# Delta-rule levels on Trainium2: the second chunk's mask chain first, the third level's masks ahead of the samples' decay, and the sample queries as a second column of the key's product

## The reference

```
L = (k k^T) * exp(where(strict, b_i - b_j, -inf)) * beta_i
U, Wk = solve((L + I), [v * beta, k * beta * exp(b)])
P = (q k^T) * exp(where(causal, b_i - b_j, -inf))
W = U - Wk S ;  o = (q * exp(b)) S + P W ;  S = exp(b_last) S + (k * exp(b_last - b))^T W
```

## Time and profile before

| What | Value |
|---|---|
| Median of 3 runs | 2649.16 us |
| The profiled execution, its own time | 2651.1 us |
| Its span, first to last instruction | 2649.4 us |
| PE busy | 2594.3 us (98%) |
| DVE, ACT, POOL busy | 1254.7 us (47%), 819.1 us (31%), 303.7 us (11%) |
| DMA | 246.75 MB, mean 93 GB/s |
| Mean granted clock of TensorE | 0.989 of full speed |

### The profile page before, as it was taken

How to read it: one execution, slowest core, us unless ns; L and a number is a source line. 1 busy time by engine, 2 the same in 40 slices (tenths; PEclk the granted TensorE clock), 3 DMA queues, 4 the chain that set the end, 5 groups by cost and what they waited for, 6 DMA issues and landing times.

```text
span 2649.4 us, 48882 instructions
## 1 busy us (share of the span) xinstructions
PE 2594.3 (98%) x20695; PEld 2501.5 (94%) x20695; DVE 1254.7 (47%) x1578; ACT 819.1 (31%) x1042; POOL 303.7 (11%) x311
## 2 busy tenths in 40 slices
PE   8999999999999999999999999999999998999998
PEld 8999999898989899999999999989998998999998
DVE  5444324647464754443344442386457645444422
ACT  4222222324232432222222222253333334322222
POOL 1000001202020210000100000104420442000000
PEclk9999999999999999999999999999999999999999
DMA  4333233525252423322333323321122111333232
GB/s 135 90 95 85 79 106 124 187 80 187 80 187 80 150 82 95 95 80 88 103 104 83 95 79 96 99 80 35 49 78 73 35 49 52 83 92 95 76 89 76
DMA packets 340334, 246.75 MB, mean 93 GB/s; under 512 B 9428, under 2 KB 320908, under 8 KB 340208
## 3 DMA queue, kind: packets, MB, share of 16 engines
q1 hardware_dynamic: 325856, 197.32, 25.2%
q0 software_dynamic: 14352, 47.58, 5.0%
HBM read 218.81 MB, written 26.05 MB: 92 GB/s over the span
## 4 chain that ended last, share of the span: by engine, by line
PE 90%; DVE 5%; issue 2%; ACT 1%; POOL 1%; DMA 0%; DVEq 0%; SPq 0%; POOLq 0%; ACTq 0%
PE ps L744 60%; PE ps L931 16%; PE ps L1119 4%; PE ps L829 1%; PE ps L850 1%; PE ps L1059 1%; PE ps L1129 1%; POOL osum L589 1%; DVE xl L1661 1%; PE ps L1070 1%; PE ps L784 1%; DVE wl L1655 1%; PE ps L1100 0%; PE ps L1082 0%; PE ps L990 0%
## 5 line engine op out<-in xcount | busy, mean ns | idle before, releaser
L744 PE MATMUL ps<-xh,wh 128*128 128x260 f32 x2816 | 569.0, 283 | 2.7 <-DVE gate L2219 1.6
L744 PE MATMUL ps<-xh,wl 128*128 128x260 f32 x2816 | 568.1, 283 | 0.0
L744 PE MATMUL ps<-xl,wh 128*128 128x260 f32 x2816 | 567.4, 283 | 0.0
L1655 DVE TENSOR_TENSOR wl<-raw,wh 128x2048 fp32r<-128x2048 f32 (+1 forms) x204 | 427.5, 2096 | 267.9 <-ACT wh L1332 267.7
L1332 ACT ACTIVATE wh<-raw 128x2048 fp32r<-128x2048 f32 (+1 forms) x204 | 354.5, 1738 | 344.0 <-PE ps L744 190.0
L744 PEld LDWEIGHTS ps<-xh,wh 128*128 128x128 f32 x2816 | 435.4, 189 | 4.7 <-issue 2.3
L744 PEld LDWEIGHTS ps<-xh,wl 128*128 128x128 f32 x2816 | 435.0, 189 | 0.0
L744 PEld LDWEIGHTS ps<-xl,wh 128*128 128x128 f32 x2816 | 433.8, 189 | 0.0
L744 PE MATMUL ps<-hh,wh 128*128 128x260 f32 x1408 | 284.4, 283 | 0.0
L744 PE MATMUL ps<-hh,wl 128*128 128x260 f32 x1408 | 283.0, 282 | 0.0
L744 PE MATMUL ps<-hl,wh 128*128 128x260 f32 x1408 | 282.8, 282 | 0.0
(11 more groups left out here) (366 smaller groups left out, 2910.6 us busy)
## 6 DMA issues: line engine op xcount, KB each, us to landing
raw<-in_ffn_gu_dram SPq DMA_DIRECT2D x176, 512.0 KB, 4.9
raw<-in_ffn_down_dram SPq DMA_DIRECT2D x64, 384.0 KB, 3.6
raw<-in_ret_w_in_dram SPq DMA_DIRECT2D x48, 512.0 KB, 4.4
raw<-in_ffn_down_dram SPq DMA_DIRECT2D x64, 320.0 KB, 4.0
s_ring<-in_state_ret_dram POOLq DMA_DIRECT2D x32, 512.0 KB, 7.0
out_dram<-s_ring POOLq DMA_DIRECT2D x32, 512.0 KB, 3.1
raw<-in_gdn_w_in_dram SPq DMA_DIRECT2D x32, 512.0 KB, 4.5
raw<-in_ret_w_out_dram SPq DMA_DIRECT2D x16, 512.0 KB, 4.1
```

What stands on the lines that cost most here:

```text
L744: m_ = nc.tensor.matmul(ps[:, 2 * q + h, 0:HALF], w_, v[:, kt0 + t, h * HALF:(h + 1) * HALF], start=b_, stop=e_)
L1655: nc.vector.tensor_tensor(wl[:, s, 0:cols], raw[:, s, 0:cols], wh[:, s, 0:cols].bitcast(F32), ALU.subtract).then_inc(w_low, 1)
```

## The change

The diff has three parts. First, the second chunk of a pair: `n1` of it is made by DVE (before, by POOL); ACT makes `d1` before the key rows `kb`, `kd`; its `pt` and `qd` and PE's `qk` stand behind level 1 and the samples' key products. The first chunk's `qd` stands behind the second's `n2`. Second, POOL makes the masks of level 3 before it scales the first two states, and those of level 5 before the other two. Third, the samples' queries: DVE copies keys and queries side by side once for each head group (`kc`, `qc`) and multiplies them (`kq`); PE's product at level 1 takes both columns, and one product with ones sums `kq` over the rows; DVE builds the output from these (`sa`, `sd`, `so`), and the products `os` and copies `oz` are gone. Beside these, the output's `o` does all four products with the state first and waits for `W` behind them.

```
             if l == 1:
+                out += [f"{n}.{both[1]}" for n in odd.split()]
...
-    pairs((["0 dd n2 L l0 m0 pt qd", "1 dd n2 L l0", "0 a1", "1 m0", "0 a2", "1 pt qd"],
+    pairs((["0 dd n2 L l0 m0 pt", "1 dd n1 n2", "0 qd", "1 L l0", "0 a1", "1 m0", "0 a2"],
...
-    pairs((["0 n1 l1", "1 n1", "0 l2", "1 l1"], ["0 n1 l1", "1 n1", "0 l2", "1 l1"]), ["l"], ["s2"], {2: ("", (0, 1), "se"), 4: ("", (2, 3), "se")})]))
+    pairs((["0 n1 l1 l2", "1 l1"], ["0 n1 l1 l2", "1 l1"]), ["l"], ["s2"], {3: ("", (0, 1), "se"), 5: ("", (2, 3), "se")})]))
...
                             for h in range(GG):
-                                m_ = nc.tensor.matmul(ps[:, 1, h * GC + b % GC:h * GC + b % GC + 1], g_ring[:, b % RING, h, :],
-                                                      gk[:, h, SEQ + b:SEQ + b + 1], start=True, stop=True)
+                                o = 2 * (h * GC + b % GC)
+                                nc.tensor.matmul(ps[:, 5, o:o + 2], g_ring[:, b % RING, h, :], pairs_s[:, h, b, :], start=True, stop=True)
                         if step == 2:
+                            m_ = nc.tensor.matmul(ps[:, 5, 2 * GG * GC:3 * GG * GC].rearrange("p (h b) -> p h b", h=GG), ones[:],
+                                                  kq[:, :, GC * p:GC * p + GC], start=True, stop=True)
                             did(m_, f"r{p}")
...
-                            v(f"wc{p}" if l == 2 else f"oz{b - 2}")
+                            v((f"pt.{2 * p + 1}" if b % 2 else f"sd{p}") if l == 2 else f"kw{b - 2}")
                             rows_of(5 - 4 * (b % 2), lambda h: wt[:, h, b:b + 1], ident[:], f"wr{b}")
-                    if l in (3, 5) and step:
-                        for b in (GC * p + l - 4 + step,):
-                            v(f"sn{b}")
-                            for h in range(GG):
-                                m_ = nc.tensor.matmul(ps[:, 5 - 4 * (b % 2), h:h + 1], g_ring[:, b % RING, h, :],
-                                                      gq[:, h, SEQ + b:SEQ + b + 1], start=True, stop=True)
-                            did(m_, f"os{b}")
...
-                        v(f"W.{c}")
                         v(f"qd.{c}")
                         for h in range(GG):
-                            o = ps[:, bb + 1, h * P:(h + 1) * P]
-                            nc.tensor.matmul(o, gs[:, h, :], ch["eb"][:, h, :], start=True, stop=False)
-                            m_ = nc.tensor.matmul(o, ch["u"][:, h, :], ch["d2"][:, h, :], start=False, stop=True)
+                            nc.tensor.matmul(ps[:, bb + 1, h * P:(h + 1) * P], gs[:, h, :], ch["eb"][:, h, :], start=h == 0, stop=False)
+                        v(f"W.{c}")
+                        for h in range(GG):
+                            m_ = nc.tensor.matmul(ps[:, bb + 1, h * P:(h + 1) * P], ch["u"][:, h, :], ch["d2"][:, h, :],
+                                                  start=False, stop=h == GG - 1)
...
+                        did(tt(s_, products[:, :, :, 1], eab[:, 0, h0:h0 + GG, at_], ALU.mult), f"sa{p}")
                         v(f"wc{p}")
+                        q_ = gq[:, :, SEQ + first:SEQ + first + GC]
+                        did(tt(q_, dots, w_, ALU.mult), f"sd{p}")
+                        v(f"sd{p}")
+                        did(tt(q_, q_, s_, ALU.add), f"so{p}")
...
+                        did(nc.vector.tensor_copy(pairs_s[:, :, :, 0], gk[:, :, SEQ:NTOK]), "kc")
+                        did(nc.vector.tensor_copy(pairs_s[:, :, :, 1], gq[:, :, SEQ:NTOK]), "qc")
+                        did(tt(kq, gk[:, :, SEQ:NTOK], gq[:, :, SEQ:NTOK], ALU.mult), "kq")
```

More of the change, by code:

```diff
@@ L93, with pairs @@
 GDN_WORDS = 24560
-def pairs(before, level, late, samples=None, early={}, norm={}):
+def pairs(before, level, late, samples=None, norm={}, odd=""):
     out = []
@@ L112, in pairs @@
                     out += [n for n in mine if n not in out]
-                    if group == "a" and l in early and c % 2 == 0:
-                        out += [f"os{GC * p + b}" for b in early[l]]
             if samples and l in samples:
@@ L163 @@
     "dq3 dq4 dq5 dq6 dq7",
-    pairs((["0 dd n2 L l0 m0 pt qd", "1 dd n2 L l0", "0 a1", "1 m0", "0 a2", "1 pt qd"],
[L165 to L168, removed]
+    pairs((["0 dd n2 L l0 m0 pt", "1 dd n1 n2", "0 qd", "1 L l0", "0 a1", "1 m0", "0 a2"],
+           ["0 L l0 m0 pt", "1 dd n1 n2", "0 qd", "1 L l0", "0 a1", "1 m0", "0 a2"]), ["a"], ["W S"], odd="pt qd", samples={1: ("wa wb wc sa sd so", (), ""), 2: ("", (0, 1), "kw sn"), 4: ("", (2, 3), "kw sn")},
+          norm={"m0.0": "kc qc kq", "W.1": "dd.2 n2.2", "m0.3": "ssA", "level4": "rnA", "level5": "rhA rlA", "last level": "yA0 yA1", "level6": "yzA0 yzA1 loA0 loA1",
                 "S.2": "xa0", "W.3": "xa1", "S.3": "xa2"}),
@@ L439, in value_bank @@
             return b if b < RING else 4 + b % 2
-        wt = ssq[:, 0:GG * DEC].rearrange("p (h b) -> p h b", h=GG)
+        wt, kq, decayed_o = (ssq[:, n * GG * DEC:(n + 1) * GG * DEC].rearrange("p (h b) -> p h b", h=GG) for n in range(3))
+        pairs_s = ssq[:, 3 * GG * DEC:5 * GG * DEC].rearrange("p (h b two) -> p h b two", h=GG, two=2)
         dg = [sq[:, n, 0:GG * P].rearrange("p (h n) -> p h n", h=GG) for n in range(2)]
@@ L670, in gdn_body @@
                                 level_of(l, c, ch)
-                        if l in (2, 4):
-                            for b in range(GC * p + l - 2, GC * p + l):
+                        if l in (3, 5):
+                            for b in range(GC * p + l - 3, GC * p + l - 1):
                                 pool.wait_ge(g_landed[b % RING], 32 * g + 16 * p + 16)
@@ L1526, in gdn_body @@
                     key_rows(*both[0])
[L1527 removed]
+                    lower_decays(*both[0])
+                    last_rows(*both[0])
+                    value_rows(*both[0])
+                    upper_decays(*both[0])
                     if p:
@@ L2010, in sample_step @@
                         w_, at_ = wt[:, :, first:first + GC], slice(first, first + GC)
-                        r_ = ps[:, 1, 0:GG * GC].rearrange("p (h b) -> p h b", h=GG)
-                        did(tt(w_, r_, eab[:, 0, h0:h0 + GG, at_], ALU.mult), f"wa{p}")
+                        products = ps[:, 5, 0:2 * GG * GC].rearrange("p (h b two) -> p h b two", h=GG, two=2)
+                        dots = ps[:, 5, 2 * GG * GC:3 * GG * GC].rearrange("p (h b) -> p h b", h=GG)
+                        s_ = decayed_o[:, :, at_]
+                        did(tt(w_, products[:, :, :, 0], eab[:, 0, h0:h0 + GG, at_], ALU.mult), f"wa{p}")
                         v(f"wa{p}")
@@ L2026, in sample_step @@
                             did(tt(g_ring[:, b % RING], g_ring[:, b % RING], dg[b % 2], ALU.add), f"sn{b}")
-                    if l in (3, 5):
-                        for b in range(first + l - 3, first + l - 1):
-                            t_(f"os{b}")
-                            did(nc.vector.tensor_copy(gq[:, :, SEQ + b], ps[:, 5 - 4 * (b % 2), 0:GG]), f"oz{b}")
                 def inverse(name):
@@ L2063, in decays @@
                         v(f"dd.{c}")
+                        if c % 2:
+                            did(tt(ch["d1"][:], ch["dd"][:], every(biglo), ALU.add), f"n1.{c}")
                         did(tt(ch["d2"][:], ch["dd"][:], every(negup), ALU.add), f"n2.{c}")
```

59 lines of the change are left out of this document (38 added, 21 removed).

## The result

The changed kernel takes 2622.1 us (median of 4 runs, 2621.5 to 2623.13) against 2649.79 us of the kernel before beside it (4 runs, 2646.99 to 2654.3): ratio 0.9897, 95% interval 0.9885 to 0.9909. That is 27.7 us less. The prediction said 2633, 16 us less, with a range from 2625 to 2641: the direction and the products' share were right, the size was not. The profiled execution took 2623.13 us, its span is 2621.4 us and its mean granted clock 0.993, where the kernel before had 0.989.

The account below looks back on a forecast made before the run. TensorE, busy 98% of the span, was taken as the bound. 13.6 - 0.9 + 2.2 + 1.0 = 15.9 us off; 2651.1 - 15.9 - 1.9 (profiled execution to median) = 2633.3, said as 2633 us, range 2625 to 2641.

Parts of the forecast that it names:

- What bounds the kernel: Whole kernel: TensorE, busy for 98% of the span, so a product taken off it comes off the time almost whole.
- the prediction's two terms: Samples' part: 13.6 us off for the query products `os`, 0.9 us added for the product with ones.
- The second column: Samples' key products at level 1: nothing taken for a second column; between 1 and 128 columns under 1 us.
- Mask chain: Second chunk up to the key products: `L` 0.9 us earlier, about 0.25 us won in four places, 1.0 us.
- Output: Output's `o`: four products with the state fill TensorE's wait for `W`, 2.2 of 2.4 us off.
- Copies and GpSimd's order: `kc`, `qc`, `kq` fit VectorE's idle time, `kq` 0.98 us if meeting GpSimd; GpSimd's order nothing, ends 2 us either way.
- The clock: the step that failed: Four stretches from the key products: four falls kept, 10.2 us lost, 1.7 us less than in the profiled execution.
- the sign of being wrong that the prediction named: Whole kernel: a mean clock off 0.989 by more than 0.003 would show the prediction wrong.
- The clock no longer falls: Rival at the key products: without the 0.22 us wait the clock loss returns, 2623 us; chance 0.07.
- Late VectorE at level 3: Rival behind `r`: VectorE's 9 to 10 us against TensorE's 9.5; at most 6.8 us given back, 2640 us; chance 0.12.
- cover by `os`: Rival at levels 3 and 5: `os` only covered waits, 13.6 us come back, 2647 us; chance 0.05.
- The lasting low clock: Rival behind the key products: half clock until level 4, 35 us more, 2668 us; chance 0.04.

Follow-up runs that it names:

- e2: The kernel before with the samples' part alone (two columns, product with ones, new output steps, no `os` and `oz`), all orders old: 2635.58 us, ratio 0.9955.
- e1: The changed kernel with one column instead of two in the samples' key products: 2623.85 us, ratio 0.9908.
- e11: The changed kernel with GpSimd's old order, scaling the states ahead of the masks of levels 3 and 5: 2623.81 us, ratio 0.9909.
- e9: The changed kernel with one more TensorE wait ahead of the key products, for ScalarE's copy of the second chunk's `t1`: 2637.76 us, ratio 0.9955.
- e10: The kernel before with its key products in the first chunk's bank, without the 0.22 us wait for the second's `pt`: 2642.35 us, ratio 0.9973.
- e5: The changed kernel with each sample's key products (8 instructions) spread behind `t1` and the first `a` of both chunks: 2615.12 us, ratio 0.9875.
- e12: The kernel before with only its key products spread among dense ones, one sample at a time, in the first chunk's bank: 2633.09 us, ratio 0.9940.
- e3: The kernel before with only the second chunk's new order of mask chain and `qk`, key products (one column) in bank 5: 2644.64 us, ratio 0.9983.
- e7: The changed kernel with only `qk` moved, from behind the key products to between `t` and `a` of level 2: 2622.14 us, ratio 0.9911.
- e8: The kernel before with only the output's new order, four products with the state first, then the wait for `W`: 2647.32 us, ratio 0.9997.
- e6: The changed kernel with key products spread one sample at a time and `qk` between `t` and `a` of level 2: 2614.08 us, ratio 0.9872.

## Why the prediction was wrong in size

*What bounds the kernel* held: TensorE's products came off the time whole. `os` was priced at 13.6 us and gave 13.9 in the trace, and e2, with the samples' part alone, gave 12.9 where the prediction's two terms make 12.7. Levels 3 and 5 became as dense as level 4. The second column cost nothing (e1), the product with ones 0.22 us a pair.

*Mask chain.* The mechanism was as told: VectorE no longer waits for ScalarE before `L`. It came 1.13 us earlier against `t1`, where I had 0.9, and the key products came 7.19 us behind `t1`, where I had 7.6. Besides the earlier `L`, the size was off because a wait of 0.22 us in the idle column is 0.39 us by the starts (1.28 against 0.89 us): the column leaves out a part of what a wait costs.

*Output.* The same: the 2.4 us of the idle column were 3.1 by the starts. The lesson of both is that the starts on either side of a wait price it, not its bracket.

*Copies and GpSimd's order.* `kq` took 0.18 us, in the cover that I had named, although GpSimd's `la` had begun 0.02 us before it; by these rows it didn't wait that step out, and the 0.98 us that I had allowed for such a meeting didn't come. GpSimd's new order is worth 1.4 us of waits (e11), inside the 2 us that I had bounded.

*The clock: the step that failed.* It was "The products that go before it stay, so I keep four falls". The products did stay, and two falls remained in the profiled execution, 6.8 us at half clock instead of 23.8. For the change itself this term was nothing (its 1.7 us stand for the way from the profiled execution to the median); it was 7.6 us in the four stretches of the profile, and over the runs the mean clock rose from 0.990 to 0.994, which is about 11 us. That is the sign of being wrong that the prediction named, a mean clock off 0.989 by more than 0.003. I had priced the wait for `pt` ahead of the key products at its own 0.22 us and looked for the fall's cause inside the low stretch, where TensorE never paused. The experiments put it ahead of the stretch. Adding a wait of half a microsecond there brought back all four falls (e9: 15.7 us for 2.1 us of waits); taking the old one away took 10.2 us of half clock with it (e10). Filling the waits with the key products themselves, and so thinning these, ended the falls in the four stretches of both kernels (e5, e12). The rival "The clock no longer falls", at 2623 us, came within 1 us of the time, at a chance of 0.07; the runs show it in part (two falls left) with work worth about 2 us more than I had.

The Trainium skill (TensorE: Matmul & The Clock Gate, section "HAM oscillation — how this bites in real kernels") lets the clock fall after idle gaps between bursts. The case it tells of has waits for a DMA that are longer than the products between them; the wait of 0.22 us here isn't one of those, so the prediction leant on the rule too far when it called the rival likely by it. I then set the rival aside on the row. The runs show more than that rule: with products of few columns behind them, waits of 0.2 to 0.5 us ahead change how often and how long the clock falls (e9, e10). The waits of 0.49 us before `a1` and 0.60 us before the turn have no such products straight behind them, and between 1821.02 and 1828.21 of the changed kernel the clock is never low. Few columns aren't needed either, if the wait is long: behind the delta rule of the changed kernel the clock is low after a wait of 3.28 us between products with 264 columns, and there the trace agrees with the rule.

```profile
2218.78 0.59 PE L1039 MATMUL ps<-gyh,wh 128*128 128x264 f32 x1 [3.28 <-DVE x L2196]
```

```profile
2219.00:2221.00 2.00, 2.00 (x10) 2.00 (x11) 1.10 (x2) 1.36 (x3) 0.91 (x1) 0.50 1.12 328
```

*The other rivals.* Late VectorE at level 3 and cover by `os` are out: 1.78 us from `a` to the turn, with no wait. The lasting low clock is out: where it fell it came back within 3.4 us.

*What stays open.* A missing wait makes the falls rarer, it doesn't exclude them: e3 has none, the same order as the changed kernel, and four falls, 17.0 us at half clock in all; e10 shows falls and none on the same code, and e7's executions differ. Nor does the wait account for all of the clock's part: taking it away gave some 6 us through the clock (e10, mean clock 0.990 to 0.992), the whole change about 11. The parts alone gave 12.9 (e2), 3.8 (e3) and 0.7 us (e8), 17.4 in all; the other 10.3 of the 27.7 us come only when they stand together, most of it through the clock (23.8, 17.0 and 27.2 us at half each alone, 6.8 together), and no run shows which of them it takes. Where a stretch lies in time may matter, but no run moved a stretch in time alone, so this is argued and not shown. Nor was it tried whether in e5 and e12 the filled waits or the thinner key products decide. The 2.7 us ahead of the delta rule are a difference between two executions of the same code.

## What to carry to other kernels

Before a run of products with few columns, read the granted clock of that stretch, and price a wait ahead of it by what the clock does behind it, not by its own length. Spread such products over the places where TensorE waits anyway: this gave 15.8 us in the old kernel without removing an instruction, and 7.0 us in the new one. Price a wait by the starts on both sides of it, and a moved step by what it does to the waits ahead of sensitive work.

## What the runs showed of the hardware

- A product with 1 and with 2 moving columns takes the same time, 1.71 us for 16 instructions; 128 columns take 1.79 us.
- Four waits of 0.54 us ahead of such products (e9) cost 15.7 us, mostly through TensorE's clock (1.2 instead of 2.4 GHz for 27.2 us instead of 6.8).
- The fall can show late: in the changed kernel the key products run at full speed, and `qk` with 128 columns behind them takes 1.81 us instead of 0.90.
- Few-column products in pieces of 8 instructions among dense ones left the clock at 2.4 GHz (e5, e6, e12: 0 us at half); the same products in pieces of 16 let it fall for 6.8 us in the changed kernel and for 27.2 us in e9, and not at all in the profiled execution of e7.
